# Layer norm of a two-layer hybrid backbone: the square of the next chunk placed directly behind the root on ScalarE

## What is computed

```python
def layer_norm(x, g, b):
    x = x.astype(jnp.float32)
    xc = x - jnp.mean(x, -1, keepdims=True)
    return xc * lax.rsqrt(jnp.mean(xc * xc, -1, keepdims=True) + NORM_EPS) * g + b
...
        x_lat = layer_norm(DN_ALPHA * x_lat + m_lat[2] * y_lat, ln_g[l, 0], ln_b[l, 0])
        f_lat = swiglu(modulate(x_lat, m_lat[3], m_lat[4]), w_ffn_in[l], w_ffn_out[l])
        x_lat = layer_norm(DN_ALPHA * x_lat + m_lat[5] * f_lat, ln_g[l, 1], ln_b[l, 1])
```

## Time and profile before

| | |
|---|---|
| median of 3 runs | 4148.32 us (4141.9 to 4148.87) |
| the profiled execution, its own time | 4146.43 us |
| its span (first to last instruction) | 4145.0 us |
| busy TensorE / VectorE / ScalarE / GpSimd | 90% / 43% / 26% / 5% of the span |
| granted TensorE clock, mean | 0.945 of full |

### The profile page before, as it was taken

One profiled execution on the slowest core, in us unless ns is written; L12 is line 12 of the kernel. 1 busy time (PEld: TensorE's weight loads), 2 busy tenths in 40 slices (PEclk: granted clock), 3 DMA queues, 4 the chain that ended last, 5 costly groups with the idle time before them and its releaser, 6 DMA issues. The chain is left out here.

```text
span 4145.0 us, 52262 instructions
## 1 busy us (share of the span) xinstructions
PE 3721.5 (90%) x22354; PEld 2997.6 (72%) x22354; DVE 1767.1 (43%) x1933; ACT 1066.2 (26%) x1473; POOL 208.4 (5%) x118
## 2 busy tenths in 40 slices
PE   7998568979889999999998999468978989999997
PEld 5887446458767888888886888336467768888886
DVE  3112857656343332332325212757656343333334
ACT  2000422456233111111114100422455141111113
POOL 0000003012000000000000000002021000000000
PEclk9999769989999999999999999679989989999998
DMA  8433540031421111111103632340042211111211
GB/s 247 107 86 113 187 154 19 13 103 44 161 92 46 31 31 45 46 30 30 46 20 122 147 91 102 130 152 11 11 123 84 85 46 46 46 46 46 61 35 41
DMA packets 294824, 318.74 MB, mean 77 GB/s; under 512 B 42398, under 2 KB 261130, under 8 KB 294410
## 3 DMA queue, kind: packets, MB, share of 16 engines
q1 hardware_dynamic: 269034, 267.43, 21.6%
q0 software_dynamic: 6912, 30.15, 2.4%
q10 hardware_dynamic: 18720, 18.88, 1.4%
HBM read 247.78 MB, written 71.59 MB: 77 GB/s over the span
## 5 line engine op out<-in xcount | busy, mean ns | idle before, releaser
L566 PE MATMUL psum<-h_hi,lead_hi 128*128 128x512 f32 (+1 forms) x1432 | 392.4, 369 | 14.8 <-DVE h_lo L1090 8.7
L566 PE MATMUL psum<-h_lo,lead_hi 128*128 128x512 f32 (+1 forms) x1432 | 390.4, 368 | 0.0
L566 PE MATMUL psum<-h_hi,lead_lo 128*128 128x512 f32 (+1 forms) x1432 | 390.1, 368 | 0.0
L1213 DVE SCALAR_TENSOR_TENSOR y<-psum,mods,y 128x1024 f32<-128x1024 f32 (+1 forms) x264 | 260.4, 1014 | 259.9 <-PE psum L566 259.0
L566 PEld LDWEIGHTS psum<-h_hi,lead_hi 128*128 128x128 f32 x1432 | 251.5, 190 | 63.2 <-DVE h_lo L1090 9.7
L1178 ACT CAST f_whi<-lead_raw 128x1024 fp32r<-128x1024 f32 x44 | 46.3, 1053 | 945.1 <-PE psum L566 934.5
L566 PEld LDWEIGHTS psum<-h_hi,lead_lo 128*128 128x128 f32 x1432 | 251.1, 190 | 45.9
L566 PEld LDWEIGHTS psum<-h_lo,lead_hi 128*128 128x128 f32 x1432 | 251.2, 190 | 45.7
L566 PE MATMUL psum<-h_hi,w_hi 128*128 128x512 f32 (+1 forms) x856 | 229.0, 369 | 37.6 <-DVE w_lo L827 26.5
L1226 DVE TENSOR_TENSOR f_hid<-f_silu,psum 128x1280 f32<-128x1280 f32 (+1 forms) x44 | 59.6, 1354 | 460.8 <-PE psum L566 336.2
L716 DVE COPY lin_stage<-psum 128x1280 f32<-128x1280 f32 (+1 forms) x48 | 68.9, 1435 | 438.3 <-PE psum L566 438.3
(11 more groups left out here) (280 smaller groups left out, 6187.1 us busy)
## 6 DMA issues: line engine op xcount, KB each, us to landing
lead_raw<-in_w_ffn_in SPq DMA_DIRECT2D x88, 512.0 KB, 6.2
ada_w<-in_w_ada SPq DMA_DIRECT2D x30, 1024.0 KB, 11.3
lead_raw<-in_w_in SPq DMA_DIRECT2D x48, 512.0 KB, 5.3
proj_cm<-lin_stage POOLq DMA_DIRECT2D x38, 640.0 KB, 4.2
f_raw<-in_w_ffn_out SPq DMA_DIRECT2D x44, 512.0 KB, 3.8
ada_w<-in_w_ada ACTq DMA_DIRECT2D x18, 1024.0 KB, 5.6
na_qk<-proj_cm SPq DMA_DIRECT2D x48, 320.0 KB, 7.6
hg_pj<-proj_cm SPq DMA_DIRECT2D x20, 640.0 KB, 9.3
```

Source lines behind the costliest of these rows:

```text
L566: ins = nc.tensor.matmul(out[:, t0:t0 + tn], w, h[:, t0:t0 + tn], start=start and n == 0, stop=stop and n == 2)
L1213: ins = nc.vector.scalar_tensor_tensor(out=y[:, o, t0:t1], in0=sets(o + 1)[:, t0:t1], scalar=gate[:, o, m:m + 1], in1=y[:, o, t0:t1], op0= ...
```

## The change

In ScalarE's loop the call of `square(i + 1)` is moved up: from behind the modulated blocks (or, in the last norm, behind `new_x`) and the first `mod_copy` of the round to directly behind `root(i)`. Nothing is added or removed, and the lists of the other engines stay as they are.

```diff
@@ -990,6 +990,8 @@
                 for i in range(n_c + (2 if last else 1)):
                     if i < n_c:
                         root(i)
+                    if i + 1 < n_c:
+                        square(i + 1)
                     if 1 <= i <= n_c and last:
                         act.wait_ge(s_u.h, s_u.at(i))
                         new_x(i - 1, KB, s_x)
@@ -998,8 +1000,6 @@
                             modulated(i - 1)
                     if i < n_c:
                         mod_copy(2 * i)
-                    if i + 1 < n_c:
-                        square(i + 1)
                     if i >= 1 and not last:
                         upper(i - 1)
                         new_x(i - 1, XA, s_xa)
```

## The result

The changed kernel takes 4112.9 us (median of 4 runs, 4111.12 to 4113.83) against 4145.11 us of the kernel before (4 runs, 4138.2 to 4148.87): a ratio of 0.9923, 95% interval 0.9909 to 0.9938. The profiled execution took 4113.32 us, its span is 4111.9 us, 33.1 less than the 4145.0 of before.

What follows compares the result with a forecast made beforehand. It took as bound the norms' ring of root, modulated blocks, copy, square, variance, modulation piece and copy. Gains of 9.2 + 9.4 + 2.4 + 8.9 = 29.9 us off 4148.3 gave 4118.4, rounded to 4118, range 4110 to 4128.

Steps and rivals of the forecast that it cites:

- The four terms of the sum: Gains forecast for the first, second, third and last norm: 9.2, 9.4, 2.4 and 8.9 us, together 29.9.
- root(0) to root(4) of the layer-0 norms: First and second norm, first to last root: shortened by the early squares, to 45.2 or 45.3 us.
- the wait of squares 3 and 4: ScalarE in the layer-0 norms: idle about 1.8 us before these squares until VectorE has centred their chunk.
- the new ring: Later layer-0 rounds: square, modulated blocks and copy, upper, lower, centre, square; 12.5 us, where the old one took 13.57.
- the term of the first norm: First layer-0 norm: root(4) comes at 1245.1 instead of 1254.29, 9.2 us earlier.
- One of the signs: Layer-0 norms: from the first mean to root(4) 57 us instead of 66, as evidence that the forecast is right.
- rival B: Variances on TensorE: the clock does not come back, variance(1) still takes 5.41; gains 24.6 us, time 4124; chance 0.14.
- Rival C: End of the layer-0 norms: TensorE takes over, lead piece 1 starting behind the turning; gains 21.3 us, time 4127; chance 0.08.
- Rival D: All norms: the early place only becomes a wait for the centre; 5 us gained, time 4143; chance 0.04.
- Rival E: Layer-0 modulation pieces: weight loads issued later behind waiting squares; at 17 us per load 12 us slower, 4160; chance 0.02.

Runs made afterwards that it cites:

- experiment 2: Changed kernel's early square kept only in part, against the kernel before: layer-0 norms alone 0.9944, last norm alone 0.9976, layer-0 round 0 alone 0.9974, layer-0 later rounds alone 0.9977.
- experiment 4: Kernel before plus unused products on TensorE ahead of each variance of the layer-0 norms, square order unchanged: 4129.83 us, ratio 0.9971.
- experiment 5: Changed kernel plus unused products on TensorE in round 3 of the layer-0 norms, ahead of piece 6 and variance(4): 4117.83 us, ratio 0.9931.
- experiment 3: Changed kernel with the square behind the modulated blocks again from round 2 on, in the three norms having them: 4118.74 us, again 4117.84 us.

## Why the prediction was right

The forecast was 4118 us in a range of 4110 to 4128; measured are 4112.9 and, the second time, 4115.7. Of the 5 us below the forecast 3.2 come from its start: it began at 4148.3 for the kernel before, and the comparison has 4145.11.

**The chains.** The four terms of the sum were 9.2, 9.4, 2.4 and 8.9; the traces have 9.57, 9.82, 2.28 and 8.97, and experiment 2 shows the layer-0 norms and the last one apart, each with its own term. 29.9 were forecast and 30.6 found. The step that was mis-sized most is root(0) to root(4) of the layer-0 norms: 44.87 instead of 45.2 or 45.3. It worked because every wait of the new order was named with what stands in front of it; the wait of squares 3 and 4 was put at 1.8 and is 1.95, the new ring at 12.5 and is 12.45.

**Where luck has a part.** The terms were differences from one trace of the kernel before. Against its second trace the same four gains are 7.62, 9.79, 2.41 and 9.46, 29.3 in sum: the term of the first norm would have been 1.6 too high, since variance(1) happened to be fast there. One of the signs also missed: from the first mean to root(4) of the first norm are 58.3 us and not 57, in both traces of the changed kernel. It lies in front of root(0), in the first two means, which took 8.83 us against the 7.14 of the trace that the prediction was read from. The second trace of the kernel before has 8.83 too, so it does not need the change.

**The clock.** "TensorE has no wait ahead of variances 1 and 2" and the full clock for them held in all four norms (3.62 or 3.72 us), so rival B did not come. But the prediction took the slow clock of the old kernel as a fixed property of its waits ("all variances behind a wait were slow"). That was wrong as a reading of its own trace, where variance(2) of the last norm waits 2.84 us and runs at full clock:

```profile
4109.54 3.72 PE L1025 MATMUL psum<-ln_sq,mean_d 128*128 128x256 f32 x16 [2.84 <-ACT ln_sq L952]
```

And it is not a fixed property: after the same 2.53 us of waiting variance(1) took 5.41 in one trace and 3.72 in the next. Nor is 1.7 us the most that a slow one costs: the 6.63 of the earlier trace rows is 2.9 above 3.72. The Trainium skill (TensorE: Matmul & The Clock Gate, section on what is happening) states that the number of slow products with which one kernel starts differs from run to run. It says so of a kernel's start; the traces here show a difference of the same kind in the middle of one, of 1.7 us for variance(1).

**What part the clock had.** The prediction counted it only in round 0 and in rival B's 24.6. Experiment 4 shows how much of the gain in the layer-0 norms is a matter of slow variances: with all variances fast, the old order has 47.36 us, and the changed order 44.87. Of the 9.6 to 9.8 us per norm some 7.1 to 7.3 can be had by the clock alone, and 2.5 are left for the order as such. The change gets there in two ways. Variances 1, 2 and 3 turn fast (5.41 to 3.72, 5.1 us in all); variance(4) stays slow and is taken off the ring, where experiment 5 shows that its length no longer counts. In the last norm the order is the larger part: step 2 loses 3.1 us with a variance of 3.72 in both kernels, and of the 5.9 that step 3 loses, variance(3) gives 2.9 (6.57 to 3.72).

**Rival C** came by half. In the changed kernel lead piece 1 of the first norm starts at 1258.90 behind the turning and runs at the lower level (0.63 us for a row's product, before 0.39). Lower(3) was over at 1258.56, so it starts 0.3 late; lead piece 2 starts at 1267.01, 0.6 behind the end of lower(4), and that is all it costs here:

```profile
1254.80 4.24 PE L302 MATMUL psum<-c_pick,ada_rows 128*128 128x2 f32 x31
1258.90 0.77 PE L566 MATMUL psum<-h_hi,lead_hi 128*128 128x512 f32 x1
1259.47 0.63 PE L566 MATMUL psum<-h_lo,lead_hi 128*128 128x512 f32 x1
```

From root(4) to the next stage are 20.46 us in the first norm against 21.51 before, where lead piece 2 stood 2.15 us at a wait for lower(4); in the second it is 21.51 in both. **Rival D** is out by the table of steps, but it has its place: rounds 2 and 3 gain only 1 us each against a slow variance, and against a fast one they lose: 12.46 in place of 11.67 and 11.59 in experiment 4. **Rival E** did not come: no wait of the changed kernel's norms was ended by a load, whose landing times are the 5.1 to 10.7 us of the earlier trace rows again.

**What stays open.** The medians say 32.2 us less in the first comparison, and the ratio of the second (0.9919) means 33.6. The stretches give 30.6 against the first trace of before and 29.3 against the second (169.1 less 139.8). The 2 to 4 us between lie outside the stretches, where two traces of before have 3974.6 and 3978.2 and two of after 3972.1 and 3974.5. The ends of the first three norms, from the last root to the next stage, explain little of it: 64.4 and 64.5 us in sum before, 64.3 and 62.9 after, with 1.0 to 1.5 less in the first norm and, in one trace of the two, 1.0 more in the third. The outside times don't separate, but they don't exclude a small effect on the stages behind the norms either; I have no experiment that does.

## What to carry to other kernels

On an in-order engine an instruction that another engine waits for goes ahead of work that nobody waits for yet, even if it then stands at a wait of its own, as long as the ring through that wait is shorter than the one it replaces; write both rings down with the steps of the trace before moving anything. Then look at what ends the new wait: here the centre on VectorE stood behind two steps that could wait, and moving it took another 10.6 us out of the four stretches.

If TensorE waits inside a ring, its clock is in the ring too, and a product that costs 3.7 us in one execution costs 5.4 in the next. An order that keeps TensorE's work off the ring, or without a gap in front of it, can be worth more than its steps say. Here it also made the layer-0 stretches repeat to 0.01 us, where those of the old order differ by up to 1.95 between two traces. And take the steps of the kernel before from more than one trace: a single one does not show which of its products might have run at the other level.

## What the runs showed that was not expected

- The same program, with the same waits to 0.01 us, ran the same product in 3.72 or 5.41 us: variance(1) of the kernel before after 2.53 us of waiting, variance(3) of experiment 3 after 3.46 us. The second is the larger part of the 2.4 us by which that norm moved.
- Additional products that nobody needs made the kernel before faster by 0.3% (ratio 0.9971, 0.9959 to 0.9982), by 7.1 to 7.3 us in each of the two norms that had them, against the first trace of the kernel before.
- In the run that moved the first square alone, variance(2) took 3.72 us instead of 5.41 in both layer-0 norms, though its own wait was still 2.51 us. One trace has this, and it doesn't show a cause.
